# A transformer layer with a PEER expert stage: first quarter of two query heads first, indices handed over in halves, gathers in another order

## The reference

```python
q = (xb @ w_query).reshape(PEER_BLOCK, PEER_HEADS, 2, PEER_QDIM // 2).astype(jnp.float32)
sc = jnp.einsum('thpd,hpkd->thpk', q, sub_keys.astype(jnp.float32))
sv, si = lax.top_k(sc, PEER_TOPK)
cand = (sv[:, :, 0, :, None] + sv[:, :, 1, None, :]).reshape(PEER_BLOCK, PEER_HEADS, PEER_TOPK * PEER_TOPK)
cidx = (si[:, :, 0, :, None] * N_KEYS + si[:, :, 1, None, :]).reshape(...)
top_s, pos = lax.top_k(cand, PEER_TOPK)
idx = jnp.take_along_axis(cidx, pos, axis=-1)
g = jax.nn.softmax(top_s, axis=-1)
a = jax.nn.gelu(jnp.einsum('thkd,td->thk', expert_u[idx], xb).astype(jnp.float32))
return jnp.einsum('thk,thkd->td', (g * a).astype(xb.dtype), expert_v[idx])
```

## Time and profile before

| what | value |
|---|---|
| median of 3 runs | 1854.15 us (1852.88 to 1854.96) |
| profiled execution, its own time | 1858.54 us |
| span of the profiled execution | 1856.7 us |
| granted TensorE clock, mean | 0.981 |
| TensorE busy | 1565.3 us (84%) |
| VectorE busy | 1097.8 us (59%) |
| GpSimd busy | 842.4 us (45%) |
| ScalarE busy | 406.3 us (22%) |

### The profile page before, as it was taken

How to read it: one execution, slowest core, us unless ns; L and a number is a source line. 1 busy time by engine, 2 the same in 40 slices (tenths; PEclk the granted TensorE clock), 3 DMA queues, 4 the chain that set the end, 5 groups by cost and what they waited for, 6 DMA issues and landing times.

```text
span 1856.7 us, 16305 instructions
## 1 busy us (share of the span) xinstructions
PE 1565.3 (84%) x5478; PEld 922.6 (50%) x5478; DVE 1097.8 (59%) x1526; ACT 406.3 (22%) x586; POOL 842.4 (45%) x1091
## 2 busy tenths in 40 slices
PE   8999999999987989987777767777777777877897
PEld 8998888789643444443322223222222223323486
DVE  6667645556766555656555555655556665554755
ACT  4435445332111010110111011011101101111254
POOL 1000000002666666756666756666666656566400
PEclk9999999999988999999999999999999999999999
DMA  7445535767999999999999999999999999999952
GB/s 256 159 147 171 180 120 177 276 218 277 411 405 415 421 419 422 420 421 418 421 422 421 421 422 421 422 422 422 422 422 423 422 422 421 422 405 422 389 195 78
DMA packets 130630, 648.38 MB, mean 349 GB/s; under 512 B 14156, under 2 KB 14264, under 8 KB 64264
## 3 DMA queue, kind: packets, MB, share of 16 engines
q0 software_dynamic: 74640, 542.41, 70.6%
q1 hardware_dynamic: 55728, 105.09, 16.7%
q10 hardware_dynamic: 200, 0.06, 0.0%
HBM read 645.42 MB, written 2.10 MB: 349 GB/s over the span
## 4 chain that ended last, share of the span: by engine, by line
PE 31%; POOL 31%; issue 19%; DMA 15%; DVE 2%; ACT 1%; POOLq 0%; DVEq 0%; ACTq 0%; SPq 0%
PE acc L1595 16%; DMA v_ring<-in_peer_v_dram,idxv 13%; POOL v_ring L490 9%; POOL u_ring L483 9%; POOL tick L489 8%; PE acc L1626 4%; POOL tick L482 3%; DMA u_ring<-in_peer_u_dram,idxu 2%; PE mix L1595 2%; PE acc L1914 2%; PE mix L1914 2%; PE acc L1812 1%; POOL u_ring L496 1%; PE mix L1669 1%; PE acc L1612 1%
## 5 line engine op out<-in xcount | busy, mean ns | idle before, releaser
L1364 DVE CUSTOM_DVE_ANT_0 u_ring<-u_ring,xn 128x2048 f32<-128x2048 f32 x256 | 586.9, 2293 | 463.8 <-DMA u_ring<-in_peer_u_dram,idxu 462.5
L1914 PE MATMUL mix<-v_ring,diag 128*128 128x512 f32 x1024 | 484.3, 618 | 128.4 <-DMA v_ring<-in_peer_v_dram,idxv 115.7
L1914 PE MATMUL acc<-v_ring,diag 128*128 128x512 f32 x960 | 440.9, 603 | 140.2 <-DMA v_ring<-in_peer_v_dram,idxv 136.9
L1914 PEld LDWEIGHTS mix<-v_ring,diag 128*128 128x128 f32 x1024 | 192.0, 196 | 389.9 <-issue 251.0
L1914 PEld LDWEIGHTS acc<-v_ring,diag 128*128 128x128 f32 x960 | 174.0, 190 | 405.0 <-issue 221.9
L489 POOL TENSOR_TENSOR tick<-tick 128x1 f32<-128x1 f32 x224 | 197.7, 882 | 298.8 <-PE acc L1914 153.5
L816 ACT ACTIVATE diag<-ident,wgt 128x128 f32<-128x128 f32 x224 | 86.0, 398 | 766.4 <-PE mix L1914 385.4
L483 POOL DMA_INDIRECT u_ring<-in_peer_u_dram,idxu x224 | 225.6, 1007 | 35.4 <-issue 31.9
L490 POOL DMA_INDIRECT v_ring<-in_peer_v_dram,idxv x224 | 224.2, 1001 | 35.0 <-issue 6.8
L971 DVE TENSOR_TENSOR w_lo<-raw,w_hi 128x2048 fp32r<-128x2048 f32 x63 | 144.4, 2292 | 141.5 <-ACT w_hi L600 140.3
L600 ACT ACTIVATE w_hi<-raw 128x2048 fp32r<-128x2048 f32 x64 | 122.4, 1914 | 206.6 <-PE acc L1595 149.3
(11 more groups left out here) (335 smaller groups left out, 1534.0 us busy)
## 6 DMA issues: line engine op xcount, KB each, us to landing
raw<-in_w_in_dram SPq DMA_DIRECT2D x48, 1024.0 KB, 5.2
raw<-in_w_out_dram SPq DMA_DIRECT2D x16, 1024.0 KB, 5.6
raw<-in_w_ple_gate_dram SPq DMA_DIRECT2D x16, 1024.0 KB, 5.7
raw<-in_peer_query_dram SPq DMA_DIRECT2D x5, 1024.0 KB, 5.1
qw_u<-in_peer_query_dram SPq DMA_DIRECT2D x4, 1024.0 KB, 15.2
qw_v<-in_peer_query_dram SPq DMA_DIRECT2D x4, 1024.0 KB, 9.1
u_ring<-in_peer_u_dram,idxu POOLq DMA_INDIRECT x256
v_ring<-in_peer_v_dram,idxv POOLq DMA_INDIRECT x248, 14.9
```

The lines of the kernel that those rows point to most:

```text
L1364: V.tensor_tensor_reduce(out=u_ring[:, k % DEEP, :], in0=u_ring[:, k % DEEP, :], in1=xn2[:, b, :], scale=1.0, scalar=0.0, op0=ALU.mult, op ...
L1914: ins = T.matmul(pairs[j // 2][:, (j % 2) * CW:(j % 2 + 1) * CW], diag[:, k % DEEP, :], v_ring[:, k % DEEP, j * CW:(j + 1) * CW], start=Fa ...
```

## The change

TensorE does the first quarter of the query weights for head 0 and head 1 and for both blocks earlier, so that u slot 0 is reported free ahead of the rest of head 1 for block 0. VectorE finds the eight best candidates of group 0, turns them into indices and hands these over (`idx_half`), and only then finds the other eight. GpSimd starts on the first eight. It issues u gather 4 ahead of u gather 3, and VectorE forms product 4 ahead of product 3; slot 3's next gather, 7, then waits for five finished products where it waited for four. In `second_group` a v gather of group 0 now stands ahead of each of the first twelve u gathers of group 1.

```diff
--- before.py
+++ after.py
@@ -242,6 +242,7 @@
         rs_ready = sem("rs_ready")
         xn2_ready, h_ready, h_chunk = sem("xn2_ready"), sem("h_ready"), sem("h_chunk")
         idx_ready, idx_taken, idx_moved = sem("idx_ready"), sem("idx_taken"), sem("idx_moved")
+        idx_half, idx_half_taken = sem("idx_half"), sem("idx_half_taken")
         u_in = [sem(f"u_in{i}") for i in range(DEEP)]
         v_in = [sem(f"v_in{i}") for i in range(DEEP)]
         v_free_dve = sem("v_free_dve")
@@ -314,6 +315,7 @@
         EARLY = 4
         AHEAD = 8
         FIRST = TOPK // 2
+        first_order = [0, 1, 2, 4, 3] + list(range(5, TOPK))
 
         def tokens_of(phase):
             return (t_hi_gate, t_lo_gate) if phase == "G" else (t_hi, t_lo)
@@ -497,6 +499,17 @@
                         u_ring[:, k % DEEP, :], None, u_rows,
                         bass.IndirectOffsetOnAxis(idxu[:, e, k:k + 1], 0)).then_inc(u_in[k % DEEP], 16)
 
+                def first_row_u(k):
+                    if k >= DEEP:
+                        pool.wait_ge(u_free, DEEP + first_order.index(k - DEEP) + 1)
+                    elif k < DEEP - 1:
+                        pool.wait_ge(u_slot_read, k + 1)
+                    else:
+                        pool.wait_ge(q_ready, 2)
+                    nc.gpsimd.indirect_dma_start(
+                        u_ring[:, k % DEEP, :], None, u_rows,
+                        bass.IndirectOffsetOnAxis(idxu[:, 0, k:k + 1], 0)).then_inc(u_in[k % DEEP], 16)
+
                 def row_v(g, e, k):
                     pool.wait_ge(v_free, g * TOPK + k + 1)
                     nc.gpsimd.indirect_dma_start(
@@ -505,16 +518,15 @@
 
                 def first_group():
 
-                    pool.wait_ge(idx_ready, 1)
-                    nc.gpsimd.tensor_copy(idxu[:, 0, :], idxn[:, :]).then_inc(idx_taken, 1)
-                    pool.wait_ge(idx_taken, 1)
-                    for k in range(AHEAD):
-                        if k < DEEP - 1:
-                            pool.wait_ge(u_slot_read, k + 1)
+                    pool.wait_ge(idx_half, 1)
+                    nc.gpsimd.tensor_copy(idxu[:, 0, 0:FIRST], idxn[:, 0:FIRST]).then_inc(idx_half_taken, 1)
+                    pool.wait_ge(idx_half_taken, 1)
+                    for k in first_order[:AHEAD]:
+                        first_row_u(k)
                         if k == DEEP - 1:
-                            pool.wait_ge(q_ready, 2)
-                        row_u(0, 0, k)
-                        if k == DEEP - 1:
+                            pool.wait_ge(idx_ready, 1)
+                            nc.gpsimd.tensor_copy(idxu[:, 0, FIRST:], idxn[:, FIRST:]).then_inc(idx_taken, 1)
+                            pool.wait_ge(idx_taken, 1)
                             nc.gpsimd.tensor_copy(idxv[:, 1, :], idxu[:, 0, :]).then_inc(idx_moved, 1)
                     pool.wait_ge(idx_moved, 1)
                     for k in range(DEEP):
@@ -523,8 +535,8 @@
                         else:
                             pool.wait_ge(q_ready, 4)
                         row_v(0, 1, k)
-                        row_u(0, 0, AHEAD + 2 * k)
-                        row_u(0, 0, AHEAD + 2 * k + 1)
+                        first_row_u(AHEAD + 2 * k)
+                        first_row_u(AHEAD + 2 * k + 1)
 
                 def second_group():
 
@@ -532,9 +544,9 @@
                     nc.gpsimd.tensor_copy(idxu[:, 1, :], idxn[:, :]).then_inc(idx_taken, 1)
                     pool.wait_ge(idx_taken, 2)
                     for k in range(TOPK):
+                        if k < TOPK - DEEP:
+                            row_v(0, 1, k + DEEP)
                         row_u(1, 1, k)
-                        if 1 <= k < 1 + TOPK - DEEP:
-                            row_v(0, 1, k + DEEP - 1)
 
                 nc.gpsimd.memset(tick[:, :], 0.0)
                 pool.drain()
@@ -1349,9 +1361,42 @@
                             dve.wait_ge(idx_taken, g)
                         V.tensor_copy(idxn[:, :], pick[:, 0, :]).then_inc(idx_ready, 1)
 
-                def top_k(g):
-                    for n in range(STAGES):
-                        top_k_stage(g, n)
+                def first_top_k():
+
+                    cf, wf = cand[:, :, :].rearrange("p a n -> p (a n)"), wk[:, :, :].rearrange("p a n -> p (a n)")
+
+                    def indices(lo, hi, done):
+                        n = hi - lo
+                        V.max_index(ci[:, lo:hi], cv[:, lo:hi], wf if lo else cf)
+                        dve.drain()
+                        V.tensor_scalar(cij[:, 0, lo:hi], ci[:, lo:hi], 4, None, ALU.logical_shift_right)
+                        V.tensor_scalar(cij[:, 1, lo:hi], ci[:, lo:hi], TOPK - 1, None, ALU.bitwise_and)
+                        dve.drain()
+                        V.tensor_copy(cijf[:, :, lo:hi], cij[:, :, lo:hi])
+                        dve.drain()
+                        for a in range(2):
+                            part_oh = oh[:, a * n:(a + 1) * n, :]
+                            V.tensor_tensor(part_oh, cijf[:, a, lo:hi].unsqueeze(2).to_broadcast([P, n, TOPK]),
+                                            i16[:, :].unsqueeze(1).to_broadcast([P, n, TOPK]), ALU.is_equal)
+                            dve.drain()
+                            V.tensor_tensor(part_oh, part_oh, tif[:, a, :].unsqueeze(1).to_broadcast([P, n, TOPK]), ALU.mult)
+                            dve.drain()
+                            V.tensor_reduce(pick[:, a, lo:hi], part_oh, AXX, ALU.add)
+                        dve.drain()
+                        V.scalar_tensor_tensor(pick[:, 0, lo:hi], pick[:, 0, lo:hi], float(NK), pick[:, 1, lo:hi], ALU.mult, ALU.add)
+                        dve.drain()
+                        V.tensor_copy(idxn[:, lo:hi], pick[:, 0, lo:hi]).then_inc(done, 1)
+
+                    for n in range(5):
+                        top_k_stage(0, n)
+                    dve.drain()
+                    indices(0, FIRST, idx_half)
+                    dve.drain()
+                    V.match_replace(wf, cv[:, 0:8], cf, NEG)
+                    dve.drain()
+                    V.max(cv[:, 8:16], wf)
+                    dve.drain()
+                    indices(FIRST, TOPK, idx_ready)
 
                 def current_top(g):
                     V.tensor_copy(topc[:, :], cv[:, :])
@@ -1407,7 +1452,7 @@
                 normed(0)
                 take_first_scores()
                 dve.drain()
-                top_k(0)
+                first_top_k()
                 dve.drain()
                 current_top(0)
                 wait_mix(dve, "tQ3")
@@ -1416,12 +1461,12 @@
                 dve.wait_ge(score_second_taken, 1)
                 for n in range(STAGES // 2):
                     top_k_stage(1, n)
-                for k in range(TOPK):
+                for n, k in enumerate(first_order):
                     products(0, 0, (k,))
-                    if k == FIRST:
+                    if n == FIRST:
                         first_weights()
-                    if k < STAGES // 2:
-                        top_k_stage(1, STAGES // 2 + k)
+                    if n < STAGES // 2:
+                        top_k_stage(1, STAGES // 2 + n)
                 other_weights()
 
 
@@ -1862,19 +1907,21 @@
                 first_query(2)
                 first_query(3).then_inc(q_first, 1)
                 pe.wait_ge(acc_free[0], gG // 2)
-                query(1, range(0, 2), (0,))
+                query(0, range(0, 2), (1,))
                 pe.wait_ge(keyst_ready, 1)
                 pe.wait_ge(qt_first, 1)
                 score(0, (0,)).then_inc(score_first, 1)
                 last_transposes(1).then_inc(mix_ready, 1)
-                query(1, range(2, KT), (0,)).then_inc(q_second, 1)
-                query(0, range(0, 2), (1,))
+                query(0, range(2, KQ), (1,))
+                query(1, range(0, KQ)).then_inc(u_slot_read, 1)
+                query(1, range(KQ, KT), (0,)).then_inc(q_second, 1)
+                query(0, range(KQ, KQ + 2), (1,))
                 pe.wait_ge(acc_free[1], gG // 2)
                 pe.wait_ge(qt_second, 1)
                 score(1, (0,)).then_inc(score_second, 1)
-                query(0, range(2, KQ), (1,))
-                query(1, range(0, KQ), (1,)).then_inc(u_slot_read, 1)
-                for q in range(1, NQ):
+                query(0, range(KQ + 2, 2 * KQ), (1,))
+                query(1, range(KQ, 2 * KQ), (1,)).then_inc(u_slot_read, 1)
+                for q in range(2, NQ):
                     if q == NQ - 1:
                         pe.wait_ge(tq_ready, NQ + 1)
                     first_pair(q)
```

## The result

The changed kernel takes 1862.06 us (median of 6 runs) against 1853.62 us before (median of 6): ratio 1.0045, 95% interval 1.0034 to 1.0057, so slower by 8.4 us. The forecast was 1858.3, with a range from 1851 to 1861.5; the measured time lies above it.

A forecast was written before the change was run, and what follows sets the result against it. The prediction took the expert stage to be bound by DMA bytes, about 422 GB/s. Its terms, 4.9 - 1.8 + 1.1 = +4.2 us, added to a median of 1854.15 gave 1858.3 us, range 1851 to 1861.5.

The forecast's parts named there:

- What bounds the kernel: Expert stage from the tenth slice: DMA bytes at 405 to 423 GB/s; the change moves the end only by bytes not moved.
- TensorE, cost 0: Start of the expert stage: same matmuls reordered, slot 0 free at 441.1 instead of 446.9, slots 1 to 3 unchanged; cost 0.
- VectorE: Group 0 selection: first-half indices at 445.0 against 447.3, all 16 2.5 us later, product 0 at 456.3.
- First term: Start of group 0: u0's head start buys nothing, the 4-before-3 swap delays u7, u8 done at 484.9 against 480.1; +4.9 us.
- Second term: Second group, 512 to 525 us: v4 first recovers nearly all bytes lost in the dip; -1.8 us (0 to -1.9).
- Third term: Start of group 2: u0's issue is held, ends near 576.9, last byte 1.6 late; +1.1 us (0 to +2.5).
- (b): Rival at u7: issue ends by 471, the queue never empties, head start survives; -4.2 us, 1849.9; chance 0.16.
- (a): Rival: losses and gain cancel, u5 wins no race (+3.7), group 2 boundary costs nothing; +1.9, 1856.0; chance 0.32 including sub-cases.
- (c): Rival at the start: queue deep enough, +4.9 becomes 0; -0.7 us, 1853.5; chance 0.06.
- products hold no issues: Rival: gather issues not held by VectorE products, u7 ends at 474.0; sum +2.1, 1856.3; chance 0.05.

The follow-up runs named there:

- experiment 1: Changed kernel with the second group's order of before put back; ratio 1.0022 to the kernel before, 4.1 us.
- experiment 3: Changed kernel with the second group's order of before and group 0's gathers and products in natural order; ratio 0.9995 to the kernel before.
- experiment 7: Kernel before with only gather and product 4 ahead of 3 in group 0; ratio 1.0017.
- experiment 2: Kernel before with only the second group's new order; ratio 1.0025.
- experiment 4: Kernel before with only v gather 4 moved ahead of the first u gather of group 1; ratio 0.9996.
- experiment 9: Kernel before with v gathers 4 to 11 ahead of u gathers 0 to 7 of group 1, none beside u8, v12 to v15 as before; ratio 0.9995.
- experiment 6: Changed kernel with v gather 15 of group 0 back behind u gather 12 of group 1; ratio 1.0027 to the kernel before.
- experiment 5: Changed kernel, group 2 only: v's index copy made at the start of group 1, four one-element additions left out; ratio 1.0032 to the kernel before.
- experiment 8: Changed kernel with natural order in group 0 and, in the second group, only v gather 4 ahead of the first u gather; ratio 0.9988 to the kernel before.

## Why the prediction was right in its sign and wrong in its size

**What bounds the kernel.** Right: time that the stream lost in the first three groups came back at the end, 8.6 us in the stretches and 8.4 in the medians.

**TensorE, cost 0.** Right: u1 at 450.8 in the frame of before, u2 at 454.3, and VectorE stood idle only 0.27 us before its copy of head 1's scores, as it did before.

**VectorE.** Right to 0.7 us: indices of the first half at 444.9 (forecast 445.0), product 0 at 456.1 (456.3), product 5 at 472.2 (472.9).

**First term, +4.9, measured +3.6.** The mechanism was right and shown by experiments 1, 3 and 7: the head start of u0 buys nothing, and the swap makes u7 late. My walk set u7 and u8 0.8 us too late (u7 ended at 475.3, forecast 476.05). The rest, some 0.5 us, lies between my 3.9 us to a last byte and the wait for product 8, which I had not measured the same way. I had put 3.7 as the lower bound, for a case that didn't come: u5 did win its race with product 4.

**Second term, -1.8, measured -1.2.** Right in kind; experiments 2, 4 and 9 show the stretch from 512 to 525 us full. The size is uncertain: experiment 1 has B = 96.0, 0.6 less than before, with the old order. The mean of B is 96.5 over the four traces with the order of before and 95.7 over the eight others, so 0.8 less. Why not more came back wasn't tested.

**Third term, +1.1, measured +6.2.** This is the step that failed. I followed one issue to group 2, u0's, set its end at 576.9, and took the queue to hold three gathers then, one of them half done. In the changed kernel it ended at 584.2 in the frame of before, with the queue empty. In experiment 2, where the start is as before, it ended at 581.3, so 4.4 us behind the forecast by the second group's order alone. I left out what GpSimd's queue does ahead of it. First, u15 of group 1 itself: it waits for product 11, whose row now lies two gathers (5 us) later in the stream. It goes out at 573.4 in the frame of before instead of 565.7, of which 2.4 us come from stretches A and B (in experiment 2 it is 4.5 us late), and it is then held, 3.02 us where it took 0.94. Second, the two index copies and four additions of `step`: before they fell into a gap of VectorE's and took 0.2 us each, after they fell between products that follow each other, and took 4.7 us in all; two of the additions were held, 1.77 and 2.25 us, and the copies were not. For the time at which u0's issue ends the first of the two is the larger part. The end of u15's issue moved by 9.8 us, and from there to the end of u0's it is 7.8 us where it was 5.5, as before 3.1 us of those had gone into the wait for product 12. My upper bound for the term, 2.5, left room for neither, and so the range was too narrow. Experiment 6 shows that giving the gap back takes 3.8 us away, experiment 5 that leaving out operations without the gap takes 1.6. How the remaining 2.4 us of experiment 6 split between u15's issue and the held v issues isn't settled.

The sign rested on the first term, which held. The errors in size partly cancelled: the three terms were off by -1.3, +0.6 and +5.1 us.

**The rivals.** (b), the head start survives, fell at u7, the place it was set at. (a), that losses and gain cancel, fell: u5 won its race, the boundary cost 6.2 us, and the loss is 6.5 us above what (a) gave. (c), a start without cost, fell with the +3.6 of stretch A. That products hold no issues is out: the copy of 0.19 us took 2.10, an issue of 0.94 took 3.01. The Trainium skill (SBUF — State Buffer, Who interferes with whom) has GpSimd instructions that read SBUF held by a VectorE instruction with two SBUF inputs; for the copies the traces agree (2.10 us). Its inference that descriptor writing isn't held would leave the issues of gathers free, and they are held (0.94 us alone, 2.2 to 3.0 beside a product); there the measurement decides. But such an issue also takes its indices from `idxu` or `idxv` in SBUF, so it may fall under the page's rule on reads; no run here separates the two.

## What to carry to other kernels

When transfers are issued by an engine that another one holds, walk its queue through every instruction up to the next point where all is as before, small operations included; here an issue that went out 4.5 us later by the order alone, and was then held, and six operations of 0.2 us behind it cost more than the step that the change was about. In a ring, the order of issue and the order of release have to agree: taking slot 0's next row ahead of slot 3's first made the fifth product, not the fourth, open slot 3, and cost 3.6 to 4.1 us of stretch A with no gain. An earlier first transfer is worth nothing while the second still waits for the same event as before.

## What the runs showed of the hardware

A GpSimd operation of 0.19 us that meets a product of 2.29 us on VectorE is recorded with 1.8 to 2.3 us. Where products follow each other with less than 0.2 us between them, not every one of a row of such operations is held: in the changed kernel the additions at 571.62 and 573.51 were, each by a product, and the copies behind them ran in 0.19 us each in the gap before the next product. The prediction had counted this for the copy in group 0 and left it out at group 2.

The clock in the early stage moved whole executions. The mark lies at 432.2 to 432.6 us in the five traces whose granted clock is 1.00 in each 100 us up to 300, at 434.0 to 434.3 in the five with 0.98 in one of them, at 435.5 in experiment 8 with 0.98 in two, and at 437.0 in the kernel before with 0.98 and 0.97, whichever the order of TensorE's work. The 4.8 us between the two kernels' marks are more than half of what was to be measured, so two spans are compared from a common mark.
